# Gated-delta groups with 32x32 second-level tiles and a z panel cut into slices between the steps, and a feed-forward boundary in one pass

## What is computed

```python
# first block, second half: x is (512, 1024)
x  = x + rmsnorm(mix, g_post_mix)                 # norm "nA"
h2 = rmsnorm(x, g_pre_mlp)                        # norm "n2"
a  = square(relu(h2 @ w_up))                      # 1024 -> 4096
ff = a @ w_down                                   # 4096 -> 1024
x  = x + rmsnorm(ff, g_post_mlp)

# second block, first layer: 16 meta tokens ahead of the 512, 16 value heads of 128, 8 key heads
qkv, z, b, a = split(h @ w_in); qkv = silu(causal_conv4(qkv)); q, k = l2norm(q), l2norm(k)
# the reference works in chunks of 64 tokens; in each chunk and head
m    = (beta*k) @ k.T * where(strictly lower, decay, 0)
u, w = solve(I + m, [beta*v, beta*k*exp(gc)])     # unit lower triangular
attn = (q @ k.T) * decay
# then chunk after chunk
v_new = u - w @ S;  o = (q*exp(gc)) @ S + attn @ v_new;  S = S*exp(g_last) + k_dec.T @ v_new
y = (rmsnorm(o) * silu(z)) @ w_out
```

## Time and profile before

| | before |
|---|---|
| median of 3 runs | 2069.16 us (2066.18 to 2071.61) |
| the profiled execution | 2070.51 us |
| its span | 2068.7 us |
| mean granted clock of TensorE | 0.956 of 2.4 GHz |
| TensorE busy | 1910.6 us (92%) |
| VectorE busy | 1003.5 us (49%) |
| ScalarE busy | 820.0 us (40%) |
| GpSimd busy | 725.7 us (35%) |

### The profile page before, as it was taken

One profiled execution on the slowest core, in us unless ns is written; L12 is line 12 of the kernel. 1 busy time (PEld: TensorE's weight loads), 2 busy tenths in 40 slices (PEclk: granted clock), 3 DMA queues, 4 the chain that ended last, 5 costly groups with the idle time before them and its releaser, 6 DMA issues.

```text
span 2068.7 us, 30690 instructions
## 1 busy us (share of the span) xinstructions
PE 1910.6 (92%) x11709; PEld 1593.5 (77%) x11845; DVE 1003.5 (49%) x1677; ACT 820.0 (40%) x1477; POOL 725.7 (35%) x454
## 2 busy tenths in 40 slices
PE   6999999799999997988989989999978999999994
PEld 4677777578787876987989988998967767777773
DVE  6422213441321325756665765675655555555564
ACT  4555542341322224524623533452335334333332
POOL 3222244343534342560471263156124212322223
PEclk9899999999999998989989999998989999999997
DMA  5111122122323231220220131122132111111111
GB/s 185 51 51 51 62 92 93 50 83 91 112 81 101 81 102 52 77 71 11 75 73 30 58 80 42 42 80 68 32 103 61 52 42 51 61 61 50 62 51 41
DMA packets 72894, 140.18 MB, mean 68 GB/s; under 512 B 30544, under 2 KB 40016, under 8 KB 72656
## 3 DMA queue, kind: packets, MB, share of 16 engines
q1 hardware_dynamic: 72064, 134.33, 20.6%
q10 hardware_dynamic: 720, 4.33, 0.5%
HBM read 129.13 MB, written 9.50 MB: 67 GB/s over the span
## 4 chain that ended last, share of the span: by engine, by line
PE 43%; DVE 6%; POOL 5%; issue 4%; ACT 3%; DMA 0%; ACTq 0%; POOLq 0%; SPq 0%; DVEq 0%
PE ps L308 8%; PE ps L309 8%; PE ps L310 8%; PE ps L2512 3%; POOL wsp L303 2%; PE ps L2468 2%; PE ps L2475 2%; PE ps L2050 1%; POOL ov L657 1%; PE ps L2502 1%; POOL work L653 1%; PE ps L2180 1%; PE ps L2201 1%; PE ps L2325 1%; PE ps L2330 1%
## 5 line engine op out<-in xcount | busy, mean ns | idle before, releaser
L303 POOL TENSOR_TENSOR wsp<-raw,wsp 128x1024 fp32r<-128x1024 f32 x231 | 556.7, 2414 | 1228.8 <-ACT wsp L298 1228.8
L308 PE MATMUL ps<-h_split,wsp 128*128 128x264 f32 (+1 forms) x1488 | 523.2, 352 | 25.5 <-POOL wsp L303 11.2
L309 PE MATMUL ps<-h_split,wsp 128*128 128x264 f32 (+1 forms) x1488 | 510.9, 343 | 0.0
L310 PE MATMUL ps<-h_split,wsp 128*128 128x264 f32 (+1 forms) x1488 | 510.3, 343 | 0.0
L308 PEld LDWEIGHTS ps<-h_split,wsp 128*128 128x128 f32 x1488 | 288.3, 194 | 64.3 <-issue 31.1
L309 PEld LDWEIGHTS ps<-h_split,wsp 128*128 128x128 f32 x1488 | 288.3, 194 | 31.5
L310 PEld LDWEIGHTS ps<-h_split,wsp 128*128 128x128 f32 x1488 | 287.3, 193 | 32.4
L298 ACT ACTIVATE wsp<-raw 128x1024 fp32r<-128x1024 f32 x231 | 240.9, 1050 | 105.1 <-PE ps L310 103.7
L308 PE MATMUL ps<-y_split,wsp 128*128 128x512 f32 (+1 forms) x496 | 195.3, 394 | 12.9 <-DVE y_split L470 5.8
L309 PE MATMUL ps<-y_split,wsp 128*128 128x512 f32 (+1 forms) x496 | 191.6, 386 | 0.0
L310 PE MATMUL ps<-y_split,wsp 128*128 128x512 f32 (+1 forms) x496 | 191.3, 386 | 0.0
(11 more groups left out here) (353 smaller groups left out, 3084.9 us busy)
## 6 DMA issues: line engine op xcount, KB each, us to landing
...
```

What stands on the lines that cost most here:

```text
L303: pool.tensor_tensor(wsp[:, s, 1, :], raw[:, s, :], wsp[:, s, 0, :].bitcast(F32), ALU.subtract).then_inc(lo_ready, 1)
L308: pe.matmul(o, wh, xh, start=start, stop=False)
L309: pe.matmul(o, wh, xl, start=False, stop=False)
L310: return pe.matmul(o, wl, xh, start=False, stop=stop)
```

## The change

- *Masks.* Only level 4 and chunk 0 mask M into CL (seven masks in place of fifteen, three buffers in place of two). Later levels take M as it is and multiply only the tiles that count.
- *Second level.* Level 5 works on 32x32 tiles (`QUARTERS`), ScalarE copies 96 partitions of it, and VectorE subtracts in two operations.
- *Who does what.* `spread_16` moves from GpSimd to VectorE, between `turned_16` and `copy_z`. `attend_mask` and chunk 0's TN move from VectorE to GpSimd, behind the masks and, for `attend_mask`, one weight split. `attend(1)` to `attend(4)` move ahead of the steps.
- *Grams* of q move from step 2 to ahead of `project(9)`, which uses banks 2 and 3 now.
- *z panel 2* (`gate_half(2)`) is cut into sixteen slices of three matmuls, which stand around the joins from step 9 on, and behind the last join. z panel 3 goes to chunk 0, and the output tiles one chunk earlier: 0, 1 in chunk 1; 2, 3 in chunk 2; 4 in halves in chunk 3.
- *Feed-forward boundary.* Norm n2's reciprocal root is applied when an up tile is evicted (VectorE: max with 0, times root; then ScalarE squares and copies), since it is one factor for each token. The high and low halves of x times gain are made slice by slice while norm nA's result is added, the mean's matmuls stand between the matmuls of up tiles 0 and 1, tile 1 lags by three slices, and round 0 is written out apart.

```diff
-    return bool(c) and l < LEVELS - 1
...
+    return bool(c) and l == LANE_LEVEL
...
+def in_quarters(l, c):
+
+    return bool(c) and l == LANE_LEVEL + 1
...
+MASKED = [s for s, (l, c) in enumerate(STEPS) if l == LANE_LEVEL or not c]
+NM = len(MASKED)
...
+LAG = 3
+GATE_FROM = 9
...
-        CL = (quad(F, 8448), quad(AX2, 2560))
+        CL = (quad(F, 8448), quad(AX2, 2560), quad(OV, 7680))
...
-                def spread_16(c):
-                    pool.tensor_tensor(by_block(TN[c]), spread(row_w, c), block_mask(NEG_TRIL_16), ALU.mult)\
-                        .then_inc(sem("g_t16"), 1)
-                for s, (l, c) in enumerate(STEPS):
...
                     n = tokens(c)[1]
-                    if s == 0:
...
-                        pool.wait_ge(sem("g_q"), gst(g, NS, s - 1))
-                    pool.tensor_tensor(CL[s % 2][0:n, :, 0:n], M[c][0:n, :, 0:n], level_mask(l, n),
+                    if k >= 3:
+                        pool.wait_ge(sem("g_q"), gst(g, NS, MASKED[k - 3] + 1))
+                    pool.tensor_tensor(CL[k % 3][0:n, :, 0:n], M[c][0:n, :, 0:n], level_mask(l, n),
                                        ALU.mult).then_inc(sem("g_cl"), 1)
-                for j in range(10, 12 if first else 16):
...
+                def attend_mask(c):
+                    n = tokens(c)[1]
+                    a = AT[c][0:n, :, 0:n]
+                    pool.wait_ge(sem("g_at"), gst(g, CHUNKS, c + 1))
+                    pool.tensor_tensor(a, a, mats[0:n, TRI_U:TRI_U + 1, 0:n].to_broadcast([n, HG, n]), ALU.mult)\
+                        .then_inc(sem("g_at2"), 1)
...
+                for k in range(3):
+                    mask(k)
...
+                pool.wait_ge(sem("l2_done"), gst(g, 4, 4))
+                pool.wait_ge(sem("g_c0"), gst(g, 1, 1))
+                pool.tensor_tensor(TN[0][0:META, :, 0:META],
+                                   mats[0:META, IDENT:IDENT + 1, 0:META].to_broadcast([META, HG, META]),
+                                   C0[0][0:META, :, 0:META], ALU.subtract).then_inc(sem("g_t0"), 1)
...
+                pool.wait_ge(sem("g_t16"), gst(g, LATER, LATER))
+                low(8)
+                for c in range(CHUNKS):
+                    attend_mask(c)
+                for j in range(9, 12 if first else 16):
                     low(j)
...
+                gained_high(act, "n2", k, HS[:, 0, k, REAL], X[:, k, REAL], "g_pre_mlp", ready=added("nA", k))
+                norm_square(act, "n2", lambda m: X[:, m, REAL], N1, k)
+            split_high(act, P_FF + AHEAD)
             norm_rsqrt(act, "n2", N1, False)
...
+                    if m or not first:
+                        split_high(act, P_FF + AHEAD + m, r, 16)
                     if m >= 2:
-                        act.wait_ge(sem("ff_sq"), gst(r, 8, m - 1))
-                    act.activation(relu[b], PS[:, m % 4, :], ACT.Relu).then_inc(sem("ff_relu"), 1)
+                        act.wait_ge(sem("ff_lo"), gst(r, 8, m - 1))
                     act.wait_ge(sem("ff_relu"), c)
-                    act.activation(Y[:, 0, m, REAL], relu[b], ACT.Square).then_inc(sem("ff_hi"), 1)
+                    act.activation(relu2[b], relu[b], ACT.Square).then_inc(sem("ff_sq"), 1)
+                    act.wait_ge(sem("ff_sq"), c)
+                    act.activation(Y[:, 0, m, REAL], relu2[b], ACT.Copy).then_inc(sem("ff_hi"), 1)
...
+                    if in_quarters(l, c):
+                        rows = 3 * P // 4
+                        act.activation(joined(QS[s % 2][0:rows, :, :], l, 1), joined(src[0:rows, :, :], l, 1),
+                                       ACT.Copy).then_inc(sem("g_qs"), 1)
...
+            def low_ff(k):
+                gained_low(dve, "n2", k, HS[:, 1, k, REAL], X[:, k, REAL], "g_pre_mlp", HS[:, 0, k, REAL])
...
+                dve.scalar_tensor_tensor(out=N1["tmp"][k % 2], in0=mixf[:, k, :], scalar=col("g_post_mix", k),
+                                         in1=N1["rs"], op0=ALU.mult, op1=ALU.mult)\
+                   .then_inc(sem("norm_branch"), 1)
+                if k % 2 == 0:
+                    dve.wait_ge(sem("norm_branch"), nth("nA", k + 1, among=ADDS))
+                    dve.tensor_tensor(X[:, k, REAL], X[:, k, REAL], N1["tmp"][0], ALU.add)\
+                       .then_inc(sem("norm_added"), 1)
+                else:
+                    if k > 1:
+                        low_ff(k - 2)
+                    low_ff(k - 1)
+            low_ff(KT - 1)
...
+                    dve.wait_ge(used, turn(P_FF + m + 1, r, 16))
+                    if m >= 2:
+                        dve.wait_ge(sem("ff_sq"), gst(r, 8, m - 1))
+                    dve.scalar_tensor_tensor(out=relu[b], in0=PS[:, m % 4, :], scalar=0.0, in1=N1["rs"],
+                                             op0=ALU.max, op1=ALU.mult).then_inc(sem("ff_relu"), 1)
...
+                def spread_16(c):
...
+                    dve.tensor_tensor(by_block(TN[c]), spread(row_w, c), block_mask(NEG_TRIL_16), ALU.mult)\
+                       .then_inc(sem("g_t16"), 1)
...
-                    dve.tensor_copy(two(zrow[t]), acc2(6 if t else 0)).then_inc(sem("z_copy"), 1)
+                    dve.tensor_copy(two(zrow[t]), acc2((0, 2, 6, 6)[t])).then_inc(sem("z_copy"), 1)
...
                 conv_clamp(7)
                 first_m(0)
                 attend(0)
+                attend(1)
+                attend(2)
                 gated(7)
+                attend(3)
+                attend(4)
                 copy_z(0)
                 turned_16(1)
-                level_0()
-                for c in ORDER[1:LATER]:
-                    turned_16(c)
+                turned_16(2)
+                spread_16(1)
                 copy_z(1)
+                spread_16(2)
+                turned_16(3)
+                spread_16(3)
...
+                        elif in_quarters(l, c):
+                            d2 = PS[:, 2 + s % 2, :].rearrange("p (h n) -> p h n", h=HG)
+                            for a, b in QUARTERS:
+                                last = dve.tensor_tensor(U[c][a, :, b], U[c][a, :, b], d2[a, :, b], ALU.subtract)
+                            last.then_inc(sem("g_u"), 1)
...
-                    if s in (4, 5, 6, 7):
-                        attend(s - 3)
-                    if s in (8, 9, 10, 11, 12):
-                        attend_mask(s - 8)
+                    if s == 0:
+                        turned_16(4)
+                    if s == 1:
...
-                    if c in (1, 2):
-                        copy_z(1 + c)
-                    if c == 3:
-                        add_out(2)
+                    if c == 1:
+                        copy_z(3)
...
+                    if c in (1, 2, 4):
+                        add_out((0, 2, None, 5)[c - 1])
...
+                    if c in (1, 2, 3):
+                        add_out((1, 3, 4)[c - 1])
...
+                def up(m, kt):
+                    last = mm3(pe, PS[:, m, :], *panel(P_FF + m, kt), HS[:, 0, kt, REAL], HS[:, 1, kt, REAL],
+                               kt == 0, kt == KT - 1)
+                    if kt == KT - 1:
+                        last.then_inc(used, 1)
...
+                    if first:
+                        pe.wait_ge(*split_ready("n2", kt + 1))
+                    up(0, kt)
+                    if first:
+                        pe.wait_ge(sem("norm_sq"), nth("n2", kt + 1))
+                        pe.matmul(PS[:, 4, :], mat(MEAN_D), N1["sq"][kt % 2], start=kt == 0, stop=kt == KT - 1)\
+                          .then_inc(sem("norm_acc"), 1)
+                        if kt >= LAG:
+                            up(1, kt - LAG)
+                    else:
+                        up(1, kt)
+                if first:
+                    for kt in range(KT - LAG, KT):
+                        up(1, kt)
...
+                for c2 in range(1, CHUNKS):
+                    grams(6, c2, 2).then_inc(sem("g_kq"), 1)
+                pe.wait_ge(sem("g_conv"), gst(g, 8, 8))
+                project(9, 2)
...
+                def gate_slices(k):
+                    gate_half(2, k // KT, k % KT, k % KT + 1)
...
-                        pe.wait_ge(sem("g_conv"), gst(g, 8, 8))
+                        pe.wait_ge(sem("z_copy"), gst(g, 4, 2))
...
+                    if in_quarters(l, c):
+                        for h in range(HG):
+                            for x, y in QUARTERS:
+                                last = pe.matmul(PS[x, 2 + b, h * P + y.start:h * P + y.stop], TN[c][x, h, x],
+                                                 QS[b][x, h, y], start=True, stop=True)
...
+                    if s in MASKED:
+                        k = MASKED.index(s)
+                        pe.wait_ge(sem("g_cl"), gst(g, NM, k + 1))
+                        left = CL[k % 3]
+                    else:
+                        left = M[c]
...
+                    if in_quarters(l, c):
+                        for h in range(HG):
```

(35 more changed lines are left out.)

126 lines of the change are left out of this document (51 added, 75 removed).

## The result

The changed kernel took 2054.6 us (median of 14 runs, 2048.16 to 2061.02), the kernel before 2068.22 us (14 runs, 2061.65 to 2074.96). The ratio is 0.9937 with a 95% interval of 0.9920 to 0.9955. I had said 2033, 2021 to 2050: the sign was right, the size was not, and the measured time lies outside the range. 36 us less was forecast and 13.6 came.

A forecast was written before the change was run, and what follows sets the result against it. TensorE, busy 1910.6 of 2068.7 us, was taken as the bound. Step stage -10.9, chunk stage -26.2, boundary -6.1 and clock +7.5 make -35.7: 2070.5 becomes 2034.8, the median 1.35 lower at 2033, range 2021 to 2050.

The forecast's parts named there:

- To the first step: Step stage, from the end of project(8) to the first step: 8.8 us, before 10.35.
- Steps 0 to 14: Step stage, from the first step to the chunk stage's first transpose: 30.6 us at the full clock.
- steps 0 to 3: Start of the step stage, now with four spreads on VectorE: 7.5 us, with the fifth step at 16.3.
- steps 4 to 9: Step stage with the second level in 32x32 pieces: 9.9 us, before 10.59.
- the last level: End of the step stage, mask wait gone and 15 slices of three matmuls added: 13.2 us, before 10.99.
- The chunk stage: Chunks after the steps, relieved of z and output work: -4.9 in group 0, -7.1 in each other, together -26.2 us.
- The boundary: Feed-forward boundary: up tiles end at 418.6, -6.5 us; 0.1 given back in each of four rounds, so -6.1.
- The clock: Second level: the clock falls until the slices bring it back, 1.9 us a group, +7.5 us.
- My own sign of being wrong: Steps 10 to 14: a granted clock under 0.8 there would show the prediction wrong.
- All steps at the half clock: Rival, chance 0.03: clock falls in the second level and stays down to the chunk stage, 15.7 us a group, 2089.
- The slices run at the half clock: Rival, chance 0.08: slices in threes may not bring the clock back, 8.7 us a group above full clock, 2061.
- The port rule: VectorE and GpSimd lock shared ports for whole instructions, so spreads wait; its rival, chance 0.10, +11 us, 2044.

The follow-up runs named there:

- e3_block: The changed kernel with all sixteen z slices as one block of 48 matmuls between steps 10 and 11; median 2037.0 us, ratio 0.9876.
- e1_early: The changed kernel with its sixteen z slices spread from step 4 on, none behind the last join; median 2021.6 us, ratio 0.9798.
- e2_halves: The changed kernel with the second level on 64x64 tiles with masks again, the z panel's split ahead of the step 5 masks; median 2044.5 us.
- e9_order: e8_from5 with turned_16(3) moved ahead of the first spread and the second z copy on VectorE; median 2013.7 us, ratio 0.9757.
- e7_pool_spread: e1_early with the four spread_16 of a group back on GpSimd; median 2037.5 us, ratio 0.9870.
- e8_from5: e1_early with its slices from step 5 on in place of 4, one behind the last join; median 2015.0 us, ratio 0.9769.

## Why the prediction was wrong

- *To the first step.* 8.8 forecast. project(9) started 2.89 us behind project(8) and its 48 matmuls took 6.01: 8.9. Right.
- *Steps 0 to 14.* 30.6 forecast at the full clock. Group 2 of the changed kernel had 30.07. Right as a sum, with errors that cancel: steps 0 to 3 took 7.1 (7.5 forecast), steps 4 to 9 8.8 (9.9), since a 32x32 pass takes 0.44 us and not 0.58, and the last level 14.1 (13.2), since a slice between small pieces adds 0.46 us (1236.71 to 1237.89 from a q pass to the join behind a slice, 0.72 without one) and not 0.375. In the 7.1 stands a wait of 0.79 ahead of step 2, because VectorE's `turned_16` takes 1.76 us beside a mask of 1.75 on GpSimd. In group 0:

```profile
875.84 1.76 DVE L1518 TENSOR_TENSOR aux_f<-work,mats 128x512 f32<-128x512 f32 x1
...
875.30 1.75 POOL L696 TENSOR_TENSOR work<-ov,mats 128x512 f32<-128x512 f32 x1 [1.23 <-PE ps L2303]
...
877.78 0.68 PE L2303 MATMUL ps<-aux_f,ov 64*64 64x64 f32 x16 [0.79 <-POOL aux_f L696]
```

- *The chunk stage.* -26.2 forecast, -27.2 measured: 8.99 for chunk 1 of group 0 (9.4 forecast), 9.93 for chunk 3 of group 1 (10.2).
- *The boundary.* -6.5 and +0.4 forecast; -7.2 and +0.3 measured.
- *The clock.* This step failed. "I expect it to fall in the second level, until the slices have brought it back ... 3.8 us of work at half speed is 1.9 a group, +7.5." It fell where I said, but the slices between the small pieces did not bring it back: about 30 us at half speed, and 11.0 to 13.6 us more than group 2 had at the full clock in each group that fell, three of four in one profiled execution and four of four in another. In place of 7.5 the term is 38 in the first and 48 in the second. That the slices would lift the clock I had taken from 922.70 in the earlier trace rows, where 24 wide matmuls stand in a row from 919.26 on and the clock rises at the fifteenth. Such a row does lift it: in e3_block after 2.7 to 5.9 us, and in the changed kernel itself behind the last join, after 3.8 to 4.5 us in its first profile, when the steps are over. Threes between small pieces did not (seven groups of seven), sixes did in one group of four, and e1_early shows that threes do hold it where it has not fallen. My own sign of being wrong, a granted clock under 0.8 over steps 10 to 14, came: it was 0.50.
- *The rivals.* "All steps at the half clock" (0.03) described what came in each group that fell, with 15.7 us a group where 11.0 to 13.6 were measured. "The slices run at the half clock" (0.08) had half of it, slices in threes that do not bring the clock back, and its 2061 is the nearest figure to 2054.6; but it priced 8.7 us a group, since its second level was to stay at the full clock. My argument against the first, that the clock held to 907.17 before the change, was about 64x64 pieces in pairs; e2_halves shows that those can even lift a fallen clock. They are no evidence for 32x32. Both rivals were also coupled with all four groups at once; what came varies by group and execution.
- *The port rule.* "A spread would wait out whatever runs there": one operation of a group did, a `turned_16` and not a spread, for 1.1 us over its 0.63 to 0.69. On the path that was 0.5 us a group (e9_order). The four spreads back on GpSimd cost 4.6, the clock's part included (e7_pool_spread). The rule held and its weight was small here.

With the measured -27.2, -6.9 and a step stage like group 2's in all four groups (4 x 38.94 - 168.48 = -12.7) the change would have been worth 47 us. e8_from5 and e9_order, which hold the clock, are 50 us faster than the kernel before in its runs beside them (2065.3 and 2063.4 us). So that is where the expected gain was: not hidden and not lost to waits, but paid back in clock.

What stays open is why the fall skips a group now and then (group 2 in one execution of the changed kernel and in e3_block, none in another) with the same instructions ahead of it. The runs show that it does and no more. Nor does a run part the size of the 32x32 pieces from the masks that went with the 64x64 ones: e2_halves brought back both, and a wait besides. Shown is that the slices do not cause the fall, and that slices inside the second level prevent it.
